# A dilated attention's score products: one f32 product per key tile, or two fp32r products of stacked high and low parts

## The reference

```python
    s = jnp.einsum('brnqhd,brnkhd->brnhqk', qb, kw).astype(jnp.float32)
    s = s + bias.transpose(2, 0, 1)
    s = jnp.where(valid[:, None], s, NEG_INF)
    m = jnp.max(s, axis=-1, keepdims=True)
    p = jnp.exp(s - m)
    den = jnp.sum(p, axis=-1, keepdims=True)
    o = jnp.einsum('brnhqk,brnkhd->brnqhd', (p / den).astype(v.dtype), vw)
```

## Time and profile before

| | us |
|---|---|
| median of 3 runs | 2792.48 (2790.01 to 2794.37) |
| the profiled execution's own time | 2793.15 |
| its span | 2791.4 |
| TensorE busy | 2641.2 (95% of the span) |
| VectorE, ScalarE, GpSimd busy | 1351.2, 836.0, 251.5 |
| mean granted TensorE clock | 0.978 of full |

### The profile page before, as it was taken

How to read it: one execution, slowest core, us unless ns; L and a number is a source line. 1 busy time by engine, 2 the same in 40 slices (tenths; PEclk the granted TensorE clock), 3 DMA queues, 4 the chain that set the end, 5 groups by cost and what they waited for, 6 DMA issues and landing times.

```text
span 2791.4 us, 28672 instructions
## 1 busy us (share of the span) xinstructions
PE 2641.2 (95%) x11363; PEld 2088.6 (75%) x11363; DVE 1351.2 (48%) x1585; ACT 836.0 (30%) x1083; POOL 251.5 (9%) x269
## 2 busy tenths in 40 slices
PE   5999999989999999999999988898999999999996
PEld 3887667867888888888765766665878888888884
DVE  5242666356334343345748878786453232232333
ACT  3211345333112021121325575435332021120221
POOL 0000222002111121121001000211000000000000
PEclk9999999999999999999899998999999999999997
DMA  3211110214222222231310111001111111111111
GB/s 111 89 46 50 42 55 32 68 60 151 91 80 87 76 90 83 76 105 61 136 41 5 46 39 39 4 8 50 67 38 53 46 46 53 45 53 45 46 53 68
DMA packets 50376, 169.68 MB, mean 61 GB/s; under 512 B 7544, under 2 KB 11128, under 8 KB 50232
## 3 DMA queue, kind: packets, MB, share of 16 engines
q1 hardware_dynamic: 32544, 104.27, 11.4%
q0 software_dynamic: 17728, 63.98, 6.7%
HBM read 152.05 MB, written 12.68 MB: 59 GB/s over the span
## 4 chain that ended last, share of the span: by engine, by line
PE 81%; DVE 9%; ACT 5%; issue 4%; DMA 0%; SPq 0%; DVEq 0%; POOL 0%; ACTq 0%; POOLq 0%
PE G L1219 61%; PE G L1237 4%; PE G L1413 2%; PE TP L1642 2%; ACT TK L1071 2%; PE G L1560 1%; PE TP L1433 1%; PE TP L1386 1%; PE TP L1257 1%; DVE JUNK L2245 1%; PE G L1576 1%; ACT T L1057 1%; PE TP L1280 1%; PE TP L1438 1%; DVE wlo L1715 1%
## 5 line engine op out<-in xcount | busy, mean ns | idle before, releaser
L1219 PE MATMUL G<-XH,whi 128*128 128x512 f32 x1712 | 539.2, 396 | 15.2 <-DVE wlo L1715 13.1
L1219 PE MATMUL G<-XL,whi 128*128 128x512 f32 x1712 | 529.9, 391 | 0.0
L1219 PE MATMUL G<-XH,wlo 128*128 128x512 f32 x1712 | 529.8, 391 | 0.0
L768 ACT ACTIVATE whi<-raw 128x1024 fp32r<-128x1024 f32 x184 | 193.8, 1053 | 732.6 <-PE G L1219 671.0
L1219 PEld LDWEIGHTS G<-XH,whi 128*128 128x128 f32 x1712 | 319.8, 189 | 86.5 <-DVE wlo L1715 15.2
L1219 PEld LDWEIGHTS G<-XL,whi 128*128 128x128 f32 x1712 | 322.7, 189 | 67.8
L1219 PEld LDWEIGHTS G<-XH,wlo 128*128 128x128 f32 x1712 | 322.7, 188 | 67.8
L1219 PE MATMUL G<-UH,whi 128*128 128x512 f32 x1024 | 316.9, 391 | 0.0
L1219 PE MATMUL G<-UL,whi 128*128 128x512 f32 x1024 | 315.6, 389 | 0.0
L1219 PE MATMUL G<-UH,wlo 128*128 128x512 f32 x1024 | 315.5, 389 | 0.0
L1715 DVE TENSOR_TENSOR wlo<-raw,whi 128x1024 fp32r<-128x1024 f32 x184 | 224.3, 1220 | 149.4 <-ACT whi L768 149.1
(11 more groups left out here) (304 smaller groups left out, 3195.2 us busy)
## 6 DMA issues: line engine op xcount, KB each, us to landing
raw<-slabs SPq DMA_DIRECT2D x184, 512.0 KB, 3.4
ADA<-ada POOLq DMA_DIRECT2D x48, 512.0 KB, 3.8
x_spill<-XT POOLq DMA_DIRECT2D x2, 4096.0 KB, 12.9
BIAS<-tab_spill POOLq DMA_DIRECT2D x8, 960.0 KB, 4.9
XT<-xT SPq DMA_DIRECT2D x8, 512.0 KB, 10.0
XRE<-xT POOLq DMA_DIRECT2D x8, 512.0 KB, 3.9
XRE<-x_spill POOLq DMA_DIRECT2D x8, 512.0 KB, 3.7
XT<-x_spill POOLq DMA_DIRECT2D x1, 4096.0 KB, 13.8
```

Of the source, the lines that this page charges most:

```text
L768: act.activation(whi[b][:, :, :].rearrange("p k n -> p (k n)"), raw[b][:, :], ACT.Copy).then_inc(hi_ready, 1)
L1219: last = pe.matmul(G[b][:, half, :], w[b][:, k, :], x[:, k, half * HALF:(half + 1) * HALF], start=(at_k == 0 and n == 0), stop=(at_k == KT ...
```

## The change

- `KA` and `QA` go. In fp32r there are `KH` (the rounded keys in both halves), `QHL` (the rounded queries in `own`, the queries' low part in `other`), `KLO` (the keys' low part in `own`; zeros and a row of ones in `other`) and `QHR` (the rounded queries in `own`; zeros and the guard's row in `other`). Each score tile is `KH` by `QHL` plus `KLO` by `QHR`, two fp32r products over 128 rows each, summed in PSUM. So a step has four fp32r matmuls.
- ScalarE makes four copies per head instead of two, one per step at d = 0, 1, 3, 4 (`operand`); `inverse` moves from d = 3 to d = 5 and `round_pair` from n = 10, 26 to n = 14, 30. The first head's four copies stand before the `turned_hi` copies.
- GpSimd makes the two low parts of each head (`low_parts`), each behind the copy that it needs, ahead of the row's DMAs. Its memsets become subtractions and products of the constant ones.
- `KLO` lies in the memory of `wlo`, `QHR` in that of `whi`. So slab 20 is no longer split before the attention: ScalarE takes its high part at n = 57, VectorE its low part at n = 59, and slab 21 follows the last scores. `product_pair` asks for the second slab's low part two steps later.

```diff
@@ -201,8 +201,10 @@
 
     STRIP = [at(f"STRIP{b}", [P, 2, 384], A_XT + 23552 + 3072 * b) for b in range(2)]
     ROW8 = [at(f"ROW8_{b}", [P, P], A_XT + 29696 + 512 * b) for b in range(2)]
-    KA = [at(f"KA{b}", [P, S], A_XT + 4096 * b) for b in range(2)]
-    QA = [at(f"QA{b}", [P, S], A_XH + 8192 + 4096 * b) for b in range(2)]
+    KH = [at(f"KH{b}", [P, S], A_XT + 4096 * b, F32R) for b in range(2)]
+    QHL = [at(f"QHL{b}", [P, S], A_XH + 8192 + 4096 * b, F32R) for b in range(2)]
+    KLO = [at(f"KLO{b}", [P, S], A_WLO + 4096 * b, F32R) for b in range(2)]
+    QHR = [at(f"QHR{b}", [P, S], A_WHI + 4096 * b, F32R) for b in range(2)]
     QR = [at("QR0", [P, S], A_XH, F32R), at("QR1", [P, S], A_R, F32R)]
     KR = [at("KR0", [P, S], A_XH + 4096, F32R), at("KR1", [P, S], A_R + 16384, F32R)]
     PT = [at(f"PT{b}", [P, HALF], A_XL + 2048 * b) for b in range(4)]
@@ -323,7 +325,7 @@
     strip_loaded = [sem(f"strip_loaded{b}") for b in range(2)]
     row_loaded = [sem(f"row_loaded{b}") for b in range(2)]
     rounded, operands_ready, ones_set = sem("rounded"), sem("operands_ready"), sem("ones_set")
-    zeros_set = sem("zeros_set")
+    zeros_set, lows_ready = sem("zeros_set"), sem("lows_ready")
     values_ready = sem("values_ready")
     guard_scores, guard_taken = sem("guard_scores"), sem("guard_taken")
     row_ready, row_made = sem("row_ready"), sem("row_made")
@@ -428,6 +430,7 @@
     GUARD_AHEAD = 12
     GUARD_EARLY = 10
     PV_BEHIND = 3
+    OPERAND_AT = (0, 1, 3, 4)
 
     def near_window(t):
 
@@ -589,12 +592,35 @@
         load_strips(0)
         load_strips(1)
         pool.wait_ge(turned, 16)
+        pool.wait_ge(slab_done, 1 + OUT1)
         for b in range(2):
-            pool.memset(KA[b][DH:P, :], 0.0).then_inc(zeros_set, 1)
-            pool.memset(QA[b][DH:P, :], 0.0).then_inc(zeros_set, 1)
+            other = halves(b)[1]
+            one = ones[other, :].unsqueeze(1).broadcast_to([DH, NT, P])
+            for t in (KLO, QHR):
+                pool.tensor_tensor(t[b][other, :].rearrange("p (t c) -> p t c", c=P), one, one, ALU.subtract).then_inc(zeros_set, 1)
         pool.wait_ge(zeros_set, 4)
         for b in range(2):
-            pool.memset(KA[b][DH:DH + 1, :], 1.0).then_inc(ones_set, 1)
+            row = halves(b)[1].start
+            one = ones[row:row + 1, :].unsqueeze(1).broadcast_to([1, NT, P])
+            pool.tensor_tensor(KLO[b][row:row + 1, :].rearrange("p (t c) -> p t c", c=P), one, one, ALU.mult).then_inc(ones_set, 1)
+
+        def low_parts(h):
+
+            own, other = halves(h)
+            pool.wait_ge(ones_set, 4 if h else 2)
+            if h:
+                pool.wait_ge(values_ready, max(h, 2))
+            if h > 2:
+                pool.wait_ge(att_scaled, h - 2)
+            in_class = lambda t: t.rearrange("p (c u) -> p c u", c=4)
+            pool.wait_ge(operands_ready, 4 * h + 1)
+            pool.tensor_tensor(in_class(QHL[h % 2][other, :]), by_class(QT[own, h // 2, :]),
+                               in_class(QHL[h % 2][own, :].bitcast(F32)), ALU.subtract).then_inc(lows_ready, 1)
+            pool.wait_ge(operands_ready, 4 * h + 2)
+            pool.wait_ge(lows_ready, 2 * h + 1)
+            pool.tensor_tensor(KLO[h % 2][own, ::-1], KT[own, h // 2, :], KH[h % 2][own, ::-1].bitcast(F32),
+                               ALU.subtract).then_inc(lows_ready, 1)
+            pool.wait_ge(lows_ready, 2 * h + 2)
 
         def scale_head(h):
 
@@ -614,18 +640,21 @@
             pool.tensor_copy(VONE[h % 2][:, :, h % 2 * DH:(h % 2 + 1) * DH],
                              VV[:, :, h * DH:(h + 1) * DH]).then_inc(values_ready, 1)
 
-        pool.wait_ge(ones_set, 2)
+        low_parts(0)
         pool.wait_ge(turned, 20)
         pool.wait_ge(turn_out, 16)
         for b in range(2):
             head_values(b)
             pool.memset(VONE[b][:, :, (1 - b) * DH:(2 - b) * DH], 1.0).then_inc(ones_set, 1)
         for h in range(HEADS):
+            if h:
+                low_parts(h)
             pool.wait_ge(row_made, h + 1)
             if h >= 2:
                 pool.wait_ge(st_ready, NT * (h - 1))
+            row = halves(h)[1].start
             for c in range(4):
-                pool.dma_start(QA[h % 2][DH:DH + 1, c * 2 * P:(c + 1) * 2 * P],
+                pool.dma_start(QHR[h % 2][row:row + 1, c * 2 * P:(c + 1) * 2 * P],
                                ROW8[h % 2][0:NT, c * 32:(c + 1) * 32]).then_inc(row_loaded[h % 2], 16)
             if h + 2 < HEADS:
                 pool.wait_ge(guard_taken, NT * (h + 1))
@@ -846,7 +875,8 @@
         for j in range(4):
 
             g = IN1 + S_V1 + j
-            hi_next(g, g % 2, g // 2)
+            if j < 3:
+                hi_next(g, g % 2, g // 2)
             act.wait_ge(slab_done, g + 2)
             act.wait_ge(turned, 8 if j < 2 else 8 + 2 * (j - 1))
             act.activation(TT[g % 2][:, ::-1], Gf[g % 2], ACT.Copy).then_inc(psum_free[g % 2], 1)
@@ -855,23 +885,34 @@
 
             if m == 1:
                 act.wait_ge(rounded, 2)
-                act.wait_ge(operands_ready, 4)
+                act.wait_ge(operands_ready, 8)
+                act.wait_ge(lows_ready, 4)
             if m >= 2:
                 act.wait_ge(guard_scores, 2 * NT * (m - 1))
             act.activation(KR[m % 2][:, :], KT[:, m, :], ACT.Copy).then_inc(rounded, 1)
             act.activation(QR[m % 2][:, :].rearrange("p (t c) -> p t c", c=P)[:, :, ::-1],
                            QT[:, m, :].rearrange("p (t c) -> p t c", c=P), ACT.Copy, scale=-1.0).then_inc(rounded, 1)
 
+        def operand(h, k):
+
+            own, other = halves(h)
+            if k == 0 and h < 2:
+                act.wait_ge(turned, 16)
+            elif k == 0:
+                act.wait_ge(st_ready, NT * (h - 1))
+            if k == 0:
+                act.activation(QHL[h % 2][own, :].rearrange("p (c u) -> p c u", c=4), by_class(QT[own, h // 2, :]),
+                               ACT.Copy).then_inc(operands_ready, 1)
+            elif k < 3:
+                act.activation(KH[h % 2][(own, other)[k - 1], ::-1], KT[own, h // 2, :], ACT.Copy).then_inc(operands_ready, 1)
+            else:
+                act.wait_ge(operands_ready, 4 * h + 1)
+                act.activation(QHR[h % 2][own, :], QHL[h % 2][own, :].bitcast(F32), ACT.Copy).then_inc(operands_ready, 1)
+
         def operands(h):
 
-            own = halves(h)[0]
-            if h < 2:
-                act.wait_ge(turned, 16)
-            else:
-                act.wait_ge(st_ready, NT * (h - 1))
-            act.activation(KA[h % 2][0:DH, ::-1], KT[own, h // 2, :], ACT.Copy).then_inc(operands_ready, 1)
-            act.activation(QA[h % 2][0:DH, :].rearrange("p (c u) -> p c u", c=4), by_class(QT[own, h // 2, :]),
-                           ACT.Copy).then_inc(operands_ready, 1)
+            for k in range(4):
+                operand(h, k)
 
         def guard_row(h):
 
@@ -896,12 +937,13 @@
             act.activation(OL[h % 2][other, :], OL[h % 2][other, :], ACT.Ln).then_inc(act_seq, 1)
             aseq.n += 1
             aseq.wait(act)
+            if h < 2:
+                act.wait_ge(lows_ready, 2 * (h + 3))
             act.activation(ATTN[h // 2][own, :], OL[h % 2][other, :], ACT.Exp, scale=-1.0).then_inc(inverse_ready, 1)
 
         def dilated_attention():
 
             act.preload_act_table_set("natural_log_exp_and_others")
-            operands(0)
             guard_row(0)
             operands(1)
             round_pair(1)
@@ -911,18 +953,21 @@
                     guard_row(h + 1)
                 act.wait_ge(st_taken, n + 1)
                 act.activation(PT[n % 4][:, :], PT[n % 4][:, :], ACT.Exp).then_inc(pt_ready, 1)
-                if n in (10, 26):
-                    round_pair(n // 16 + 2)
-                if n == 40:
-                    hi_next(OUT1, OUT1 % 2, OUT1 // 2)
-                if d == 1 and 1 <= h < HEADS - 1:
-                    operands(h + 1)
+                if n == NT * (HEADS - 1) + 1:
+                    act.wait_ge(st_ready, NT * (HEADS - 1))
+                    hi(OUT1, OUT1 % 2, OUT1 // 2)
                 if d == 2 and h:
                     sums_copy(h - 1)
-                if d == 3 and h:
+                if d in OPERAND_AT and 1 <= h < HEADS - 1:
+                    operand(h + 1, OPERAND_AT.index(d))
+                if d == 5 and h:
                     inverse(h - 1)
+                if n in (14, 30):
+                    round_pair(n // 16 + 2)
                 if n in (52, 60):
                     attended(n // 8 - 6)
+            act.wait_ge(st_ready, NT * HEADS)
+            hi(OUT1 + 1, (OUT1 + 1) % 2, (OUT1 + 1) // 2)
             sums_copy(HEADS - 1)
             inverse(HEADS - 1)
 
@@ -940,6 +985,7 @@
 
         act.wait_ge(slab_done, 1 + OUT1)
         round_pair(0)
+        operands(0)
         turned_hi(4, 4, 16)
         dilated_attention()
         for k in range(2, 4):
@@ -1222,7 +1268,7 @@
 
```

(30 more changed lines are left out.)

## The result

The changed kernel takes 2775.07 us (median of 4 runs, 2771.64 to 2778.26) against 2791.48 beside it (4 runs); the ratio is 0.9938, with a 95% interval of 0.9924 to 0.9952. Eight further runs of it (experiment 10) had a ratio of 0.9925 (0.9899 to 0.9951) to the runs beside them. So it is faster by some 16 us, inside the range of the prediction (2754 to 2785) and 5 us above the 2770 that it names.

What follows compares the result with a forecast made beforehand. TensorE's queue bounds most steps, ScalarE's copies the stalls at d = 3. Gains 8.8 + 0.4 + 3.1 + 2.6 + 9.9 + 0.1 = 24.9, costs 0.2 + 2.1: 22.6 us off, 2770; own range 2762 to 2778, with rivals 2754 to 2785.

Steps and rivals of the forecast that it cites:

- What bounds: First attention: TensorE's own queue bounds most steps; near scores' group falls to 0.55 us, near steps to 2.2, gaining 8.8.
- step 3: Near scores at step 3, in the first head: their shorter products gain 0.4 us.
- Far scores bound by their strided loads: Steps d = 4 to 7: four strided weight loads stay, the group goes from 1.14 to 1.02 us, gaining 3.1.
- ScalarE: One operand copy per step: d = 3 takes 3.05 us, bound by the sums' chain alone; gains 2.6, 9.9 and 0.1.
- GpSimd and the start: Before the first scores and in the loop: low parts of 2.35 us mostly covered; costs 0.2 us, bounds 0 and 5.
- The end: Output slab splits moved to steps 57 and 59 and behind the last scores: cost nothing, bounds 0 and 1 us.
- The clock at the start: Steps 0 to 2: less TensorE work brings a fall to the 0.50 clock; adds 2.1 us, bounds 0 and 4.
- Far loads that don't bind: Rival: far steps go to 2.2 us, 13 us more gained, total 2757; chance 15%.
- Scores no cheaper: Rival: a 256-column fp32r product takes 0.21 us, only the stalls' 12.6 us go, total 2780; chance 8%.
- A fall in every head: Rival: the clock falls once per head near d = 3 and 4, 13 us more, total 2783 to 2785; chance 10%.
- The slower rival: Rival: fp32r products of 256 columns cost 0.45 us each, as f32 does, total 2833; chance 5%.

Runs made afterwards that it cites:

- experiment 10: The changed kernel unaltered, run again for its spread; 2777.02 us (8 runs, 2767.32 to 2792.45), ratio 0.9925.
- Experiment 3: The changed kernel with far steps' weights read from 128 contiguous keys instead of every fourth, so without the true far scores; 2758.18 us (one run).
- 4: The kernel before the change, f32 scores, with far scores read from contiguous keys; 2804.21 us (one run), the stretch 181.4 us, 3.0 less than before.
- experiment 6: The changed kernel with the copies of the sums at d = 2 ahead of that step's exponential instead of behind it; 2767.53 us (4 runs), ratio 0.9898.
- experiment 1: The kernel before the change with only ScalarE's work moved to the new order, scores still f32; 2778.16 us (10 runs), ratio 0.9945.
- experiment 7: The changed kernel with each low part of heads 2 to 7 made twice by GpSimd; 2786.61 us (one run).
- experiment 5: The changed kernel with four products of 512 columns that nobody reads behind the scores of steps 0, 1 and 2; 2764.77 us (4 runs), ratio 0.990.
- experiment 2: The changed kernel with ScalarE's old order, all four operand copies at d = 1; 2840.57 us (one run), the stretch 237.3 us.
- 9: The changed kernel with idle products in steps 0 to 2, sums first, and each of the first eight guards made three times, not twice; 2764.47 us (5 runs).
- 8: The changed kernel with both idle products in steps 0 to 2 and the sums ahead of the exponential; 2766.48 us (6 runs), ratio 0.989.

## Why the prediction was right, and where its sizes were off

*What bounds.* Right. The near scores' group went to 0.57 where 0.55 was said, the near step to 2.22 (2.2); 21 steps x 0.39 = 8.2 us (8.8). The gain forecast for step 3 (0.4) didn't come, as the clock was at 0.5 there.

*Far scores bound by their strided loads.* Right: 1.05 (1.02), 2.69 (2.65); heads 1 to 7 give 2.0 us and d = 5 to 7 of head 0 another 0.3, where 3.1 was said. Experiment 3 shows the cause and 4 that it was nearly hidden before.

*ScalarE.* Right: d = 3 takes 3.12 (3.05). That the sums hang on their chain "alone" holds for every second head only; in heads 2, 4 and 6 ScalarE's copies end 0.02 us behind VectorE's tile (head 2), a coincidence that the prediction did not foresee, and one that took back part of experiment 6's gain. Heads 1 and 3 gained 3.7 at d = 3 and 1.1 at d = 4 each (3.8, 1.15), the others 0.4 to 0.65. Taken apart by experiment 1, the order gives 14.4 alone. On top of it the products give 8.2 near, 2.0 far, and cost 2.5 at d = 3 (2.70 to 3.12, six times, since a shorter score group leaves the chain to the sums bare) and 2.5 in head 0: 5.2 net.

*GpSimd and the start.* Right in kind: first scores 0.4 us earlier, not later. The six clearing instructions took 1.9 us each, not 2.35, the query lows 2.90; so the row's DMAs went out at 313.07, not 316.0, and the first exponential at 323.21, not 325.6. The values of step 0 waited for neither. Inside the loop the two lows of head 3 end 10.7 us behind head 2's start (9.9), and experiment 7 shows how much room is left. The end cost nothing: from step 63's scores to the output's product 4.5 us, before 4.4.

*The clock at the start.* This term was mis-sized. The prediction added 2.1 us, "bounds 0 and 4", for a fall of the length of the old ones (6.8 us). It came, and experiment 5 shows that it comes from steps 0 to 2 as said. But it lasted 10.2 us in the first trace and 27.3 in that of experiment 10, 2.7 and 9.2 us of time. Why it lasts longer at one time than at another stays open: TensorE was busy for 9.43 of 10.10 us of the short fall and 26.44 of 27.20 of the long one. That the median lies 5 us above the 2770 forecast fits such longer falls, but only the profiled runs show where their clock fell.

*The total.* The profiled execution (2771.6) lies 1 us from the forecast, and that is partly luck. Of the 22.6 us forecast the stretch gave 19.6: 22.1 in heads 1 to 7, less 2.5 in head 0, where the fall outweighs what the products gave. The other 1.8 us came before and behind the stretch (0.36 and 1.46), where the sum has no gain at all.

*The rivals.* Far loads that don't bind: excluded by 3. Scores no cheaper: excluded by the near steps. A fall in every head: not in this kernel, where the stall at d = 3 is 0.9 us; experiment 2 shows it where the stall is 4.3. The slower rival: an fp32r product of 256 columns costs 0.12 here, not 0.45.

## What to carry to other kernels

When a step of one engine gets shorter, list what its old length covered: here a chain through two other engines took back 2.5 of 10 us, and weight loads with a stride kept the far steps, half of all, at a gain of 0.1 us where the near ones had 0.4. Judge where a helper engine's work stands by the latest time at which its next urgent instruction may start, and put the long copies in the steps that have none; that was worth 14 us without any new arithmetic. A stretch that is made lighter for TensorE may lose its clock: a few products that nobody reads, put where it waits anyway, kept it in three traces of three.

## What was not expected

The time of one and the same kernel moves by some 20 us, and its mean clock with it: of the eight runs of experiment 10 the fastest (2767.32) was granted 0.980, the slowest (2792.45) 0.968. Where the clock falls is on record for the twelve traces only, and there it is around the first scores. Ahead of them it did not fall in six (1, 2, 3, 5, 6, 9), and all but 9 have them at 315.85 to 317.73 us; it fell for some 7 us in four (before, changed, 8, 10), with the first scores at 319.88 to 320.36; it fell for 37 us in two (4, 7), with the first scores at 331. In the steps behind them a fall lasted 10.2, 13.7 or 27.3 us. The runs beside it of the kernel before spread from 2787.69 to 2807.57 too, so a gain of a few microseconds is read better from the steps of a trace than from medians. Why a fall lasts long in one run and short in the next was not found.
